# Second mixer: the convolution of the delta rule moved into the turn that makes q, k and v, and the two products per level of its inverse made one

## The reference, cut to what matters

```python
qkv = silu(causal_dwconv(concat([q, k, v]), conv_w))        # 4 taps along the positions
q = l2norm(heads(q)) * HEAD_DIM ** -0.5;  k = l2norm(heads(k));  v = heads(v)
# per chunk of the positions, per head:
lmat  = where(strict, (k_beta @ k.T) * decay, 0)
t_inv = solve(eye + lmat, eye)                               # unit lower triangular
u, w  = t_inv @ v_beta, t_inv @ (k_beta * exp(g_cum))
o     = q_decay @ state + attn_intra @ (u - w @ state)
o     = rmsnorm(o, norm_g) * silu(z)
x     = x + concat([sb_out, gdn_out]) @ w_out
```

## Time and profile before

| | |
|---|---|
| median of 3 runs | 3042.76 us (3038.23 to 3044.9) |
| the profiled execution | 3031.73 us, span of its instructions 3029.9 us |
| PE busy | 2900.7 us, 96% of the span |
| DVE, ACT busy | 1990.0 us (66%), 1482.9 us (49%) |
| mean granted TensorE clock | 0.983 of full speed |
| four attention stages | 1491 to 1681 us of the span |
| four delta rule stages and the output product | 1681 to 2125 us |

### The profile page before, as it was taken

One profiled execution on the slowest core, in us unless ns is written; L12 is line 12 of the kernel. 1 busy time (PEld: TensorE's weight loads), 2 busy tenths in 40 slices (PEclk: granted clock), 3 DMA queues, 4 the chain that ended last, 5 costly groups with the idle time before them and its releaser, 6 DMA issues.

```text
span 3029.9 us, 47315 instructions
## 1 busy us (share of the span) xinstructions
PE 2900.7 (96%) x16652; PEld 2515.4 (83%) x16652; DVE 1990.0 (66%) x2756; ACT 1482.9 (49%) x1699; POOL 41.4 (1%) x65
## 2 busy tenths in 40 slices
PE   7999999998999999999899999999989999999997
PEld 6888888887888888888788878888868888888886
DVE  4777767767888888544534556666658888886443
ACT  5444444446555555434444444445555555554343
POOL 0000000000000000000000000000000000000000
PEclk9999999999999999999889999999999999999999
DMA  5444444443555555555334432324425555555553
GB/s 202 159 149 147 146 143 144 151 140 104 194 194 182 189 184 192 198 184 182 123 108 148 155 103 99 105 98 167 160 94 177 187 191 179 184 194 190 185 181 118
DMA packets 130153, 479.42 MB, mean 158 GB/s; under 512 B 14480, under 2 KB 14496, under 8 KB 129648
## 3 DMA queue, kind: packets, MB, share of 16 engines
q1 hardware_dynamic: 129600, 473.14, 46.9%
q0 software_dynamic: 432, 4.53, 0.4%
HBM read 475.51 MB, written 2.10 MB: 158 GB/s over the span
## 4 chain that ended last, share of the span: by engine, by line
PE 84%; DVE 6%; ACT 6%; issue 3%; POOL 1%; DMA 1%; DVEq 0%; SPq 0%; ACTq 0%
PE acc L355 48%; PE acc L357 25%; ACT whi L295 2%; PE ps L755 2%; PE ps L422 1%; DVE KQ L668 1%; POOL KM L1502 1%; DVE KQ L669 1%; PE ps L1207 1%; PE ps L1216 1%; PE ps L1214 1%; DVE wlo L301 1%; DMA raw<-stream 1%; DVE m L498 0%; PE ps L391 0%
## 5 line engine op out<-in xcount | busy, mean ns | idle before, releaser
L355 PE MATMUL acc<-hs,whi 128*128 128x512 f32 x5056 | 1806.5, 400 | 8.6 <-DVE hin L328 4.5
L301 DVE TENSOR_TENSOR wlo<-raw,whi 128x1024 fp32r<-128x1024 f32 x896 | 1071.2, 1222 | 658.6 <-ACT whi L295 657.4
L357 PE MATMUL acc<-hs,wlo 128*128 128x256 f32 x5056 | 1424.0, 282 | 0.0
L295 ACT ACTIVATE whi<-raw 128x1024 fp32r<-128x1024 f32 x896 | 930.8, 1054 | 844.4 <-PE acc L357 830.9
L355 PEld LDWEIGHTS acc<-hs,whi 128*128 128x128 f32 x5056 | 954.4, 189 | 233.1 <-issue 9.6
L357 PEld LDWEIGHTS acc<-hs,wlo 128*128 128x128 f32 x5056 | 957.4, 189 | 0.6 <-issue 0.5
L355 PE MATMUL acc<-acts,whi 128*128 128x512 f32 x1408 | 499.6, 398 | 0.0
L357 PE MATMUL acc<-acts,wlo 128*128 128x256 f32 x1408 | 396.2, 281 | 0.0
L355 PEld LDWEIGHTS acc<-acts,whi 128*128 128x128 f32 x1408 | 264.3, 188 | 65.2
L309 ACT ACTIVATE half<-acc 128x512 f32<-128x512 f32 x218 | 130.0, 596 | 349.7 <-PE acc L357 349.7
L357 PEld LDWEIGHTS acc<-acts,wlo 128*128 128x128 f32 x1408 | 265.4, 189 | 0.3
(11 more groups left out here) (272 smaller groups left out, 2192.9 us busy)
## 6 DMA issues: line engine op xcount, KB each, us to landing
raw<-stream SPq DMA_DIRECT2D x896, 512.0 KB, 3.4
x<-xT SPq DMA_DIRECT2D x1, 2048.0 KB, 8.1
memr<-memT POOLq DMA_DIRECT2D x1, 2048.0 KB, 9.3
outT<-sq POOLq DMA_DIRECT2D x1, 2048.0 KB, 6.5
vec<-vecs SPq DMA_DIRECT2D x1, 489.0 KB, 8.4
KQ<-masks SPq DMA_DIRECT2D x1, 448.0 KB, 10.0
cst<-consts SPq DMA_DIRECT2D x1, 256.0 KB, 9.0
neg<-consts POOLq DMA_DIRECT2D x1, 192.0 KB, 2.6
```

Source lines behind the costliest of these rows:

```text
L295: nc.scalar.activation(whi[:, b, :], raw[:, b, :], ACT.Copy).then_inc(hi_ready, 1)
L301: nc.vector.tensor_tensor(wlo[:, b, :], raw[:, b, :], whi[:, b, :].bitcast(F32), ALU.subtract).then_inc(lo_ready, 1)
L355: nc.tensor.matmul(acc[:, 2 * par + n, :], whi[:, b, c:c + P], src[:, kt, :], start=(kt == 4 * first), stop=False)
L357: mm = nc.tensor.matmul(acc[:, 2 * par + n, 0:T], wlo[:, b, c:c + P], src[:, kt, 0:T], start=False, stop=(kt == 4 * last + 3))
```

## The change

Five things are changed, all in the second mixer.

1. **Convolution earlier.** The 24 steps of convolution, `gbm` and `bbm`, the silu of q, k and v and the squares become `gd_*_in` (`take_in`) and run in the stage that makes q, k, v and z, each part after its own group. Stage t's side work is now `take_in` of turn t and the whole of turn t - 1, the output part with it. PE's `ssq` and `rows` move from slot 7 to slot 0, `kk` from 11 to 4.
2. **Level 0 without a second product.** `TT` takes level 0 from `NLT` itself and `Tm` from `y0`; `z0` and the clearing of `Y` are gone. `Tm` and `TT` are set ahead of `NLT`, and `tr` no longer waits for them.
3. **One product per level.** ACT writes y into one half of each column pair of `Z`, POOL copies the half of `TT` into the other, and PE multiplies `Z` with itself.
4. **Waits of the levels.** The next y waits for the copy into `Tm` alone; POOL's copy waits for the one into `TT`.
5. **Attention and gates.** The first product of the attention comes one PE slot later, `cs` and `o` come two to three slots later, and the second product of the gates three PE slots later, with ACT's and DVE's slots moved to match.

```diff
-            yield from pause(6)
+            yield from pause(9)
             pe.wait_ge(gt_vec.sem, gt_vec.count("g"))
...
         def sb_tensor(pe, t, par):
+            yield
             pe.wait_ge(evac, GROUP_AT["mix"] + 3 * t + 2 + 3)
...
-            yield from pause(7)
+            yield from pause(9)
             pe.wait_ge(sb_vec.sem, sb_vec.count("sp", t))
...
+        def gd_vector_in(dve, t, par):
...
+            yield from pause(5)
...
+            dve.wait_ge(evac, g + 0 + 3)
+            taps(0, 0)
+            yield
+            taps(0, 2)
+            yield from pause(3)
...
+            taps(1, 0)
+            yield
+            taps(1, 2)
+            yield
...
+            yield
+            dve.wait_ge(evac, g + 2 + 3)
+            taps(2, 0)
+            yield
+            taps(2, 2)
+
+        def gd_vector(dve, t, par):
...
+            for lv in range(1, LEVELS):
                 dve.wait_ge(gd_pe.sem, gd_pe.count(f"z{lv}", t))
...
+                if lv < LEVELS - 1:
+                    dve.wait_ge(gd_vec.sem, gd_vec.count(f"t{lv - 1}", t))
+                    keep(Tm, lv, 0, t, ps[:, 1, :])
+                dve.wait_ge(gd_vec.sem, gd_vec.count(f"tt{lv - 1}", t))
+                keep(TT, lv, 1, t, ps[:, 1, :])
                 yield
...
+        def gd_scalar_in(act, t, par):
+            yield from pause(14)
+            act.wait_ge(gd_vec_in.sem, gd_vec_in.count("v3", t))
+            nc.scalar.activation(gy[:], gy[:], ACT.Silu).then_inc(gd_act_in.sem, 1)
...
+            for lv in range(1, LEVELS):
+                pe.wait_ge(gd_vec.sem, gd_vec.count(f"t{lv - 1}", t))
...
                 pe.wait_ge(gd_act.sem, gd_act.count(f"y{lv}", t))
+                pe.wait_ge(gd_pool.sem, gd_pool.count(f"z{lv}", t))
                 for a in range(4):
-                    y, tt = Y[:, a, :], TT[:, a, :]
-                    nc.tensor.matmul(half_of(ps[:, 1, col(a)], LEVELS - 1 - lv, 0), tt,
-                                     half_of(y, LEVELS - 1 - lv, 0), start=True, stop=True)
-                    mm = nc.tensor.matmul(half_of(ps[:, 1, col(a)], LEVELS - 1 - lv, 1), y,
-                                          half_of(tt, LEVELS - 1 - lv, 1), start=True, stop=True)
+                    mm = nc.tensor.matmul(ps[:, 1, col(a)], Z[:, a, :], Z[:, a, :], start=True, stop=True)
...
+                side = slots(16 * n, take_in(eng, t, t % 2),
+                             delta(eng, t - 1, (t - 1) % 2) if t else attend(eng, 3, 1))
                 mix_stage(eng, what, 12 + 4 * t, 4, qkvz(t % 2), side)
...
+            split_product(eng, what, "mixout", mixs, delta(eng, 3, 1), x, 16, "n8", "xattn")
...
+            for t in range(4):
+                for lv in range(1, LEVELS):
+                    pool.wait_ge(gd_vec.sem, gd_vec.count(f"tt{lv - 1}", t))
...
+                    nc.gpsimd.tensor_copy(half4(Z[:].rearrange("p a b -> p (a b)"), lv, 1),
+                                          half4(TT[:].rearrange("p a b -> p (a b)"), lv, 1)).then_inc(gd_pool.sem, 1)
```

More of the change, by code:

```diff
@@ L1009, in col, with taps @@
             return slice(a * P, (a + 1) * P)
[L1011 to L1016, removed]
+        def gd_vector_in(dve, t, par):
+            g = GROUP_AT["mix"] + 12 + 4 * t
+            def taps(s, first):
+                for j in (first, first + 1):
                     for h in range(2):
@@ L1133, in gd_scalar @@
             nc.scalar.activation(DTr[:], DTr[:], ACT.Exp).then_inc(gd_act.sem, 1)
-            yield
-            yield
-            yield
-            act.wait_ge(gd_pe.sem, gd_pe.count("tr", t))
-            for h in range(2):
-                for c in range(2):
-                    ins = nc.scalar.activation(vb[:, 2 * h + c, :], ps[:, 3, col(2 * h + c)], ACT.Copy,
-                                               scale=gts[:, c, 2 * t + h:2 * t + h + 1])
-            ins.then_inc(gd_act.sem, 1)
@@ L1172, in gd_scalar_out @@
             nc.scalar.activation(o_rms, o_rms, ACT.Exp, scale=-0.5).then_inc(gd_act_out.sem, 1)
+            yield
         def gd_tensor(pe, t, par):
-            yield from pause(7)
-            pe.wait_ge(gd_act.sem, gd_act.count("sqk", t))
+            pe.wait_ge(gd_act_in.sem, gd_act_in.count("sqk", t))
             if t == 0:
@@ L1183, in gd_tensor @@
             mm.then_inc(gd_pe.sem, 1)
-            pe.wait_ge(gd_vec.sem, gd_vec.count("bbm", t))
+            pe.wait_ge(gd_vec_in.sem, gd_vec_in.count("bbm", t))
             for a in range(4):
@@ L1195, in gd_tensor @@
             yield from pause(2)
-            pe.wait_ge(gd_vec.sem, gd_vec.count("TT", t))
+            pe.wait_ge(gd_vec.sem, gd_vec.count("nl", t))
+            for a in range(4):
+                mm = nc.tensor.matmul(half_of(ps[:, 0, col(a)], LEVELS - 1, 0), NLT[:, a, :],
+                                      half_of(ident, LEVELS - 1, 0), start=True, stop=True)
+            mm.then_inc(gd_pe.sem, 1)
+            yield
             pe.wait_ge(gd_act.sem, gd_act.count("qe", t))
@@ L1202, in gd_tensor @@
             yield
-            for lv in range(LEVELS):
-                if lv:
-                    pe.wait_ge(gd_vec.sem, gd_vec.count(f"tt{lv - 1}", t))
+            for lv in range(1, LEVELS):
+                pe.wait_ge(gd_vec.sem, gd_vec.count(f"t{lv - 1}", t))
                 for a in range(4):
@@ L1247, in gd_tensor_out, with mix_all @@
             nc.tensor.matmul(ps[:, 1, :], ones, o_sq, start=True, stop=True).then_inc(gd_pe_out.sem, 1)
-        def mix_all(eng, what, gates_, attend, delta, put_out):
+        def mix_all(eng, what, gates_, attend, take_in, delta):
             n = 2 if what == "pe" else 1
```

184 lines of the change are left out of this document (93 added, 91 removed).

## The result

| | before | after |
|---|---|---|
| median of 4 runs each | 3042.86 us | 2961.83 us (2956.08 to 2965.38) |
| ratio after / before | | 0.9736, 95% interval 0.9725 to 0.9748 |
| the profiled execution, its span | 3031.73, 3029.9 us | 2958.57, 2956.8 us |
| mean granted TensorE clock | 0.983 | 0.988 |
| first product of the second mixer to the first of the norm behind it | 610.8 us | 528.8 us |

The kernel is 81 us faster, where 70.3 us were forecast; 2961.8 us lies in the range.

A forecast was written before the change was run, and what follows sets the result against it. PE was taken to bound the kernel. Gains of 28.3, 35.8 and 20.1 us, less 7.9 and 6.0 us, made 70.3 us; taken from the 3042.8 us median this gave 2972.5 us, range 2956 to 2994 us.

The forecast's parts named there:

- the `ssq` term: Delta rule: PE's wait for the squares goes, with its refills and the slow clock behind it; together 22 us gained.
- that of `kk`: Delta rule hand-over: kk waits for late k, 2.0 us in turns 1 to 3, 0.8 in turn 0; 7.9 us lost.
- A, the products: Delta rule levels: 128-column records cost no more than 64-column ones, and level 0 loses z; 28.3 us gained.
- B, the delta rule's waits: Delta rule: PE's waits of ssq and tr go, and y waits for the copy into Tm alone; 35.8 us gained.
- 7.2 for level 0: Delta rule, level 0: z goes whole, with the slowing of a half block; 7.2 us gained in 4 turns.
- C, attention and gates: Attention and gates: later products end PE's waits and the slow clock behind them; 14.8 and 5.3, together 20.1 us gained.
- D(1), the wait of `kk`: Delta rule hand-over: round_hi and take_lo delay q and k, so kk waits, sometimes with slow clock behind; 7.9 us lost.
- D(2), DVE's levels fit: Delta rule levels: DVE's copies, take_lo and taps need 4.2 us at most of each 4.6 us level, so they fit.
- D(3), POOL's copy: Delta rule levels: POOL's copy is held by take_lo and the taps, PE waits 2.0 us in three turns; 6 us lost.
- 0 if it slips in at once: Lower bound for the loss from POOL's copy in the levels, set at 6 us: 0 if the copy isn't held.
- All is hidden: Rival for the delta rule: k in time, POOL not held, nothing given back; 84 us gained, 2959 us; chance 0.15.

The follow-up runs named there:

- the second comparison: The changed kernel run once more without edits, compared with the kernel before: 2960.85 against 3037.70 us, ratio 0.9749.
- the run with two halves: Product of Z with itself made as two products of 64 columns each, against the changed kernel: 2981.83 us, ratio 0.9812 of the kernel before.
- the run with both parts back: Changed kernel with z in two products and the attention and gates moves undone: 3003.63 us, ratio 0.9871 of the kernel before.

## Why the prediction was right, and where its sizes were off

The direction and the range held, and most terms; 81 us came (77 in the second comparison) where 70.3 were summed, just outside the forecast's own 2964 to 2983 us. That it came so near is in part luck: a price of 6.0 us that did not exist and gains that were set too small lie on one side of the sum, the price of `kk` on the other. Two slips of the sum nearly cancel as well: from its own parts the `ssq` term is 22.8 us, not 22, and that of `kk` 9.0, not 7.9 (0.8 + 6.0 of wait, 0.6 of refills, 1.6 of slow clock). A refill is the 0.16 us by which a product behind a wait starts later than in a running row, where each starts that much ahead of the end of the one before. By its own steps, and for the stretch of 82.0 us between the two profiles, counted over PE's records from start to start:

- **A, the products: right.** Forecast 28.3 us; the products y and z fell from 71.3 to 42.2 us, 29.0 less. Split again, six of the seven levels cost 21.0 us, forecast 21.1 (by the records 21.5). Shown by the run with two halves.
- **B, the delta rule's waits: right in kind, perhaps some us too small.** The waits of `ssq` and `tr`, 23.0 us, are gone; `ssq` and `rows` themselves fell from 21.9 to 13.7 us, as the slow clock left them, 8.2 us; `tr` 0.9. That is 32.1 us; the plain blocks of all parts lost a further 8.2 us of slow clock and refills, of which B has a share. So B is 32 to 40 us by the records. Not in the sum at all was a wait of the output product for `x` (1.4 us before, at 2096 us), which ended too. From the other side, the run with both parts back is worth 37 to 39 us; less 7.2 for level 0, and with the 10 to 12 us of `kk` added back, B is 40 to 44 us by that, which the intervals leave uncertain by some 6 us. The 35.8 us lie inside the first account and below the second; how much of the excess is B's own is not settled.
- **C, attention and gates: right, and in both parts.** Forecast 20.1 us, measured 20.1 (put back) and 22 (alone). By the traces of the run that puts them back the attention is 14.8 us, forecast 14.8, and the gates 4.8, forecast 5.3. Between the two first profiles the gates' stretch (start of the mixer to the first `sin`) gained 10 us, but 3.4 us of that is where the clock happened to fall: it took 53.7 us in the first profile of the changed kernel and 57.1 in the second.
- **D(1), the wait of `kk`: the mechanism to the letter, the size too small.** Forecast 0.8 and three times 2.0 us; measured 1.21 and three times 2.34, and the step that scales q and k is what PE waits for. The whole price was set at 7.9 us and is 10 to 12 us by the run that removes it: 8.2 us of wait less 0.8 that stayed, and behind it a clock that fell in turns 2 and 3 where one in three had been counted. Over the ten profiles that keep this wait it fell behind 24 of the 30 waits of 2.3 us, and behind none of the ten of 1.2 us. Windows of PE in the changed kernel from `kk` to y of level 0, the same 32 records, turn 2 and then turn 1:

```profile
1868.20:1874.48 6.28, 6.28 (x32) 5.76 (x33) 5.06 (x9) 1.06 (x1) 0.43 (x1) 0.73 0.50 162
1798.36:1803.06 4.70, 4.70 (x32) 4.33 (x33) 4.18 (x7) 1.06 (x1) 0.25 (x1) 1.00 0.60 215
```

  A clock of 0.73 instead of 1.00 costs 1.6 us here, and came behind waits of the same 2.34 us.
- **D(2), DVE's levels fit: right.** Even 1.2 to 1.4 us more DVE work in six slots of a turn left PE without a wait on `wlo` in these stages.
- **D(3), POOL's copy: the term that failed, 6.0 us for 0.** The prediction took one row, the 2.39 us, and carried it to copies of another size with other DVE steps behind them. Fifteen of the 24 copies are held for 0.9 us by `take_lo` and not by the taps behind it. Held ones end 0.7 to 1.2 us before PE needs them, so nothing reached PE. The 2.39 us themselves were no accident (copies of the first mixer take them again and again), but in the levels POOL was never held for two steps. The two runs that doubled the copy and that took it off POOL measure the term as 0 (stages 312.7 and 313.0 us against 311.1 and 312.6). The prediction's lower bound, "0 if it slips in at once", was nearer: it slips in after one step.

Three runs measure the parts apart: 21.0 us for six levels' products, 20.1 for attention and gates, 37 to 39 for the rest with `kk`'s price taken off. Together they are 78 to 80 us, between the 77 and 81 of the whole. Of the rivals *All is hidden* came nearest in time (2959 us), but not as it was put: k was late, POOL was held, and the gain of the waits was larger instead.

The Trainium skill's page "SBUF — State Buffer", section "SBUF: two separate sides", calls the pair of ports of GpSimd and VectorE an exclusive lock that goes to whoever starts first. The traces agree as far as one instruction goes: POOL's 1.25 us beside `take_lo`, and DVE's 1.42 us instead of 1.22 beside POOL's copy. The page doesn't say who is next when both wait. In the levels it was POOL each time; in the first mixer it was DVE in 20 cases of 23.

## What to carry to other kernels

Where a step on the shared path between two engines is late, ask which of the waiting engine's own steps stand between its input and it: taking q and k ahead of one `round_hi` of ACT and one `take_lo` of DVE, work that was three blocks ahead anyway, was worth 10 to 12 us and is one moved line. A price taken from one odd row should be checked against what stands around it (size, the step behind, is the reader late at all?) before it is multiplied by 24. And count the margin first: fifteen of POOL's copies did lose 0.9 us each, under a cover of 1.6 us and more.

## What the runs showed of the hardware

**POOL and DVE take turns, in the levels.** There a copy of POOL waits for one DVE step from SBUF, then goes, and the DVE step behind it is slower: L1020 took 485 ns beside such a copy and 346 without, L1023 616 and 478 ns. With the doubled copy both orders show at the same place. In turn 0 POOL was 0.01 us ahead of DVE and DVE paid (0.95 us for L1092); in turn 1 DVE started with it, POOL paid (0.96 us for 0.41), and then the next DVE step (L1095, 0.63 us for 0.41). DVE and POOL timelines of the run with two copies, turn 0, then turn 1:

```profile
1734.39 0.95 DVE L1092 TENSOR_TENSOR ATr<-ATr,cst 128x512 f32<-128x512 f32 x1
1735.26 0.41 DVE L1095 TENSOR_TENSOR qd<-qd,gy 128x256 f32<-128x256 f32 x1
...
1805.15 0.69 DVE L1092 TENSOR_TENSOR ATr<-ATr,cst 128x512 f32<-128x512 f32 x1
1805.76 0.63 DVE L1095 TENSOR_TENSOR qd<-qd,gy 128x256 f32<-128x256 f32 x1
```

```profile
1734.38 0.41 POOL L1541 COPY Z<-TT 128x256 f32<-128x256 f32 x1
...
1805.15 0.96 POOL L1541 COPY Z<-TT 128x256 f32<-128x256 f32 x1
```

**PE's pace has two values at the same granted clock.** From 800 to 1200 us PE is busy throughout at a clock of 1.00 in every profile, with the same products. The changed kernel's first profile shows 2266 of them, its second 2305, and the kernel before 2305: 1.7% apart, 9 us by the end of that stretch. The windows, of the changed kernel's first and second profile:

```profile
800.00:1200.00 400.00, 400.00 (x2266) 347.36 (x2265) 325.23 (x477) 220.20 (x230) 0.00 (x0) 1.00 0.56 184
```

```profile
800.00:1200.00 400.00, 400.00 (x2305) 350.76 (x2304) 330.95 (x487) 224.08 (x234) 0.00 (x0) 1.00 0.56 189
```

From start to start a block takes 2.77 us at the one pace and 2.83 at the other. Of the fourteen profiles three (the kernel before, the changed kernel again, the copy on DVE) ran at the quick pace from about 740 us, and all three fell back to the other between 1200 and 1300 us; none was quick in the second mixer. What sets it was not looked into. At 9 us it is as large as the whole spread of the changed kernel's runs (2956.08 to 2965.38), and the reason why two profiled spans alone would have given 73 us for a change of 77 to 81.
